# Hybrid encoder trunk: products of constants placed in TensorE's waits, and short column sums spread between long products

## The reference, cut to what matters

```python
kappa = heads(k * k_k)
kh = kappa / jnp.maximum(jnp.sqrt(jnp.sum(kappa * kappa, axis=-1, keepdims=True)), 1e-12)
...
s = (s * w_t[:, :, None, :] - sk[..., None] * (a_t * kh_t)[:, :, None, :]
     + v_t[..., None] * k_t[:, :, None, :])
...
mean = jnp.mean(y, axis=-1, keepdims=True)
var = jnp.mean((y - mean) ** 2, axis=-1, keepdims=True)
y = (y - mean) * lax.rsqrt(var + RW_GN_EPS)
y = y * gn_gain + gn_bias
y = y + jnp.sum(r_h * k_h * r_k, axis=-1, keepdims=True) * v_h
return (y.reshape(bsz, t_len, BRANCH_W) * gate).astype(p.dtype)
```

## Time and profile before

| | |
|---|---|
| median of three runs | 3393.79 us |
| the profiled execution | 3399.08 us |
| its span, first to last instruction | 3397.4 us |
| mean granted clock of TensorE | 0.978 |
| TensorE busy | 3278.0 us (96%) |
| VectorE, ScalarE, GpSimd busy | 1473.5, 1180.7, 1192.4 us |
| DMA | 68 GB/s read from HBM over the span |

### The profile page before, as it was taken

The page is one execution under the profiler, slowest core; times in us unless marked ns, Lnnn a source line. Parts: engine busy times, 40 slices in busy tenths (PEclk is TensorE's granted clock), DMA queues, the critical chain, the costliest instruction groups (busy, mean ns, idle before and its releaser), DMA issues. The chain is left out here.

```text
span 3397.4 us, 72942 instructions
## 1 busy us (share of the span) xinstructions
PE 3278.0 (96%) x29406; PEld 3008.8 (89%) x29406; DVE 1473.5 (43%) x2548; ACT 1180.7 (35%) x2251; POOL 1192.4 (35%) x906
## 2 busy tenths in 40 slices
PE   9999999989899999999999999999898989999997
PEld 8999999977687999999999999999776868888886
DVE  6331155445767334332053312554467673353312
ACT  3222252324554334222242223513245543342222
POOL 4444435200012443444444443351000124545442
PEclk9999999988999999999999999999899999999999
DMA  3333222001121332333233332220021213323332
GB/s 105 90 90 90 82 71 64 6 18 50 41 55 33 89 93 73 90 90 92 74 88 92 90 89 83 66 59 4 18 54 40 58 29 99 87 82 95 93 95 70
DMA packets 464405, 236.48 MB, mean 70 GB/s; under 512 B 20862, under 2 KB 462476, under 8 KB 464156
## 3 DMA queue, kind: packets, MB, share of 16 engines
q1 hardware_dynamic: 464156, 232.92, 24.5%
HBM read 230.50 MB, written 2.10 MB: 68 GB/s over the span
## 5 line engine op out<-in xcount | busy, mean ns | idle before, releaser
L579 POOL TENSOR_TENSOR W_low<-W,W_high 128x512 fp32r<-128x512 f32 (+1 forms) x544 | 723.9, 1332 | 858.6 <-ACT W_high L659 857.9
L155 PE MATMUL PS<-u_high,W_high 128*128 128x264 f32 (+1 forms) x2832 | 864.4, 305 | 5.1 <-ACT vg L2180 1.9
L156 PE MATMUL PS<-u_low,W_high 128*128 128x264 f32 (+1 forms) x2832 | 857.8, 303 | 0.0
L157 PE MATMUL PS<-u_high,W_low 128*128 128x264 f32 (+1 forms) x2832 | 857.6, 303 | 0.0
L659 ACT ACTIVATE W_high<-W 128x512 fp32r<-128x512 f32 (+1 forms) x544 | 336.5, 620 | 984.7 <-PE PS L157 936.0
L155 PEld LDWEIGHTS PS<-u_high,W_high 128*128 128x128 f32 x2832 | 533.1, 188 | 32.4 <-issue 6.3
L156 PEld LDWEIGHTS PS<-u_low,W_high 128*128 128x128 f32 x2832 | 533.6, 188 | 21.6
L157 PEld LDWEIGHTS PS<-u_high,W_low 128*128 128x128 f32 x2832 | 531.6, 188 | 21.7
L155 PE MATMUL PS<-u_high,dW_high 128*128 128x264 f32 (+1 forms) x1344 | 407.2, 303 | 9.0 <-POOL dW_low L1752 4.6
L157 PE MATMUL PS<-u_high,dW_low 128*128 128x264 f32 (+1 forms) x1344 | 385.5, 287 | 0.0
L156 PE MATMUL PS<-u_low,dW_high 128*128 128x264 f32 (+1 forms) x1344 | 385.2, 287 | 0.0
(11 more groups left out here) (399 smaller groups left out, 5359.6 us busy)
## 6 DMA issues: line engine op xcount, KB each, us to landing
W<-in_ffn_w_in SPq DMA_DIRECT2D x352, 256.0 KB, 2.9
dW<-in_w_in SPq DMA_DIRECT2D x172, 256.0 KB, 2.9
W<-in_ffn_w_out SPq DMA_DIRECT2D x160, 256.0 KB, 2.8
W<-in_w_in SPq DMA_DIRECT2D x80, 256.0 KB, 3.0
W<-in_w_branch SPq DMA_DIRECT2D x48, 256.0 KB, 2.9
W<-in_w_out SPq DMA_DIRECT2D x32, 256.0 KB, 2.8
W<-in_ffn_w_out SPq DMA_DIRECT2D x32, 128.0 KB, 2.2
xt<-in_x SPq DMA_DIRECT2D x4, 512.0 KB, 4.8
```

The lines of the kernel that those rows point to most:

```text
L155: nc.tensor.matmul(dst, wh, xh, start=first, stop=False)
L156: nc.tensor.matmul(dst, wh, xl, start=False, stop=False)
L157: return nc.tensor.matmul(dst, wl, xh, start=False, stop=final)
L579: g.tensor_tensor(WL[:, r, 0:nk], W[:, r, 0:nk], WH[:, r, 0:nk].bitcast(F32), ALU.subtract).then_inc(S("split"), 1)
```

## The change

`token_sums` can issue one feature tile at a time, and RWKV's projections put two blocks of the input projection behind each of the first three tiles of sums; 14 blocks follow instead of 20. In the recurrence a new helper `occupy(bank, count)` issues products ones x ones of 128 columns into an unused part of a bank: two, three and three in the step of the last chunk, twice three in the last step, and four behind the loop. RWKV's output has the squares two by two around the first bonus sum, and four products ones x ones ahead of the wait for the root. The FFN that ends layer 0 gets five of them as well.

```diff
--- before.py
+++ after.py
@@ -174,9 +174,9 @@
                     sp.sem_clear(range(numbers[0], numbers[-1] + 1))
             named.clear()
 
-        def token_sums(src, weights, nw):
-
-            for m in range(4):
+        def token_sums(src, weights, nw, tiles=range(4)):
+
+            for m in tiles:
                 for j, (t0, n) in enumerate(ST_):
                     c = 4 * nw * j + nw * m
                     last = nc.tensor.matmul(PS[0:n, 0, c:c + nw], src(m)[:, t0:t0 + n], weights, start=True, stop=True)
@@ -647,7 +647,10 @@
                             pe.wait_ge(S("out_put"), KD - 3)
                             nextp.turn(pe, PS[:, 0])
                         early_sums(pe)
-                        if not nextp:
+                        if nextp:
+                            for _ in range(5):
+                                nc.tensor.matmul(PS[:, 1, 0:P], ones[:], ones[:], start=True, stop=True)
+                        else:
                             lead.occupy(pe, 5)
 
                     @block.scalar
@@ -1194,8 +1197,12 @@
                     dense.blocks(pe, 4)
                     pe.wait_ge(S("kappa_squares"), 1)
                     pe.wait_ge(S("sigmoid"), 8)
-                    token_sums(lambda m: s4[:, m], per_parity, 2).then_inc(S("kappa_sums"), 1)
-                    dense.blocks(pe, 20)
+                    for m in range(4):
+                        last = token_sums(lambda m: s4[:, m], per_parity, 2, (m,))
+                        if m < 3:
+                            dense.blocks(pe, 2)
+                    last.then_inc(S("kappa_sums"), 1)
+                    dense.blocks(pe, 14)
                     for m in range(4):
                         spread_out(m)
                         dense.blocks(pe, 8)
@@ -1522,6 +1529,12 @@
                                 last = product(zps[:, m], carry[:, m, 1], carry[:, m, 0], CH, CH)
                         last.then_inc(S("carry2_made"), 1)
 
+                    def occupy(bank, count):
+
+                        for _ in range(count):
+                            nc.tensor.matmul(PS[:, bank, 384:512], ones[:], ones[:], start=True, stop=True,
+                                             skip_group_check=True)
+
                     for g in range(NG + 1):
                         p, makes, steps = g - 1, g < NG, g > 0
                         whole, was_whole = makes and LEN[g] == CH, steps and LEN[p] == CH
@@ -1533,12 +1546,18 @@
                             read(p)
                         if makes:
                             reach_grams(g)
+                        if g == NG:
+                            occupy(0, 3)
                         if steps:
                             first_solution(p)
+                        if g == NG:
+                            occupy(0, 3)
                         if makes:
                             squares(g)
                         if was_whole:
                             second_solution(p)
+                        if g == NG - 1:
+                            occupy(7, 2)
                         if makes:
                             fourths(g)
                         if was_whole:
@@ -1548,8 +1567,12 @@
                             eighths(g)
                         if steps and makes:
                             new_state(p)
+                        if g == NG - 1:
+                            occupy(3, 3)
                         if makes:
                             inverses(g)
+                        if g == NG - 1:
+                            occupy(3, 3)
                         if steps:
                             if not was_whole:
                                 pe.wait_ge(S("x0"), g)
@@ -1561,6 +1584,7 @@
                         if whole:
                             carries(g, 1)
                             double_carries(g)
+                    occupy(0, 4)
             clear()
             rec.close()
             with nc.Block() as block:
@@ -1665,10 +1689,14 @@
 
                     for m in range(4):
                         sums(y[:, m], half_ones[:], m, "sum_y")
-                    for m in range(4):
-                        squares(m)
+                    squares(0)
+                    squares(1)
                     bonus(0)
+                    squares(2)
+                    squares(3)
                     bonus(1)
+                    for _ in range(4):
+                        nc.tensor.matmul(PS[:, 6, 0:P], ones[:], ones[:], start=True, stop=True, skip_group_check=True)
                     pe.wait_ge(S("var_rsqrt"), 1)
                     spread_out(0)
                     pe.wait_ge(S("bonus_out"), 1)
```

## The result

The kernel after takes 3400.3 us (median of 20 runs), the kernel before 3391.4 us in 20 runs of its own. One run of each took far longer (5125.57 and 4341.32 us) and stays out of the ratio; the others lie between 3393.2 and 3406.0, and between 3388.1 and 3399.6. The ratio is 1.0022 with a 95% interval of 1.0016 to 1.0028: slower by 7.5 us (5.4 to 9.5). The forecast was 3382, and its range ended at 3395.

What follows compares the result with a forecast made beforehand. TensorE, busy 96% of the span, was taken to bound the kernel, with its clock at half in places. Terms -4.8 - 0.5 + 2.2 + 0.4 - 3.6 + 1.2 - 6.4 - 0.4 = -11.9 us off the 3393.79 median gave 3382, range 3371 to 3395.

Steps and rivals of the forecast that it cites:

- Kappa: RWKV's projections: sums spread among input-projection blocks keep the clock full, -4.8 us for both layers, bounds 0 and -4.8.
- Stage change: Layer 0 to layer 1: five constants add about 0.9 us, full clock gains 1.5; net -0.5 us.
- Constants inside the recurrence: Last chunk: eight products, gross 1.7 us per layer, partly absorbed by starved issue; +2.2 us for both layers.
- Constants in the last step: Recurrence's last step: twice three products hidden in waits for ScalarE's copy but for 0.1 each; +0.4 us for both layers.
- Outputs of the last step: Recurrence's end: 48 records run at full instead of half clock, 1.8 us gained per layer; -3.6 us for both.
- closing constants: Four products behind the recurrence's loop take 0.86 us, the following gap shrinks; +1.2 us for both layers.
- Sums of y: RWKV's output: sixteen records take 3.5 us at full clock instead of 6.67; -6.4 us for both layers.
- Squares and bonus: RWKV's output: reordered squares and constants before the root gain little, as the clock may fall; -0.4 us for both layers.
- rival (c): Only kappa and stage change hold; at the recurrence's end constants delay the clock's fall: +4.2 us, 3398, chance 0.20.
- Rival (b): RWKV's output: the squares hold the clock as well, another 2.45 us gained per layer; 3377, chance 0.20.
- (d): Everywhere edited: light work between does not matter for the clock, constants bring no return; +10.4 us, 3404, chance 0.07.
- (e): Gains come but about 5 us are lost to longer half-clock stretches at the next phase's start or later; 3387, chance 0.08.

Runs made afterwards that it cites:

- the tail constants: Kernel before plus only twice three products of constants in the recurrence's last step and four behind its loop: ratio 1.0005, 3394.25 us.
- the tail held: Kernel before plus spread kappa sums, stage-change constants, last-step and closing constants, and two more between the halves of the last outputs: 1.0004, 3390.54 us.
- the output's constants: Kernel before plus only four products of constants ahead of the wait for the root in RWKV's output: ratio 1.0009, 3396.83 us.
- the pair: Kernel before plus spread kappa sums and the five stage-change constants, nothing at the recurrence's end or in RWKV's output: 0.9995, 3388.66 us.
- parted squares: Kernel before plus seven products of constants behind each of the first three groups of squares in RWKV's output: single run, 3401.8 us.

## Why the prediction was wrong

Fourteen profiles, each with two layers, let every term be read many times over. The table gives the mean of each piece, without and with its edit, and the difference for both layers (for the stage change, once), beside the forecast. In brackets the number of cases; a kernel with only a part of a piece's edit, or with another one there, is left out of its row. The pieces: kappa from its first sum to its first spreading product; stage change from the first transpose to the first long product; last chunk from its first square to the last step's read of the state, last step from there to the first output; outputs to the first sum of y, the closing constants included; y sums to the first squares; from there to the next phase's first product.

| piece | without, us | with, us | measured | forecast |
|---|---|---|---|---|
| kappa | 21.67 (20) | 19.00 (8) | -5.3 | -4.8 |
| stage change | 10.78 (10) | 10.39 (4) | -0.4 | -0.5 |
| last chunk | 9.22 (22) | 10.82 (6) | +3.2 | +2.2 |
| last step | 2.25 (20) | 2.84 (6) | +1.2 | +0.4 |
| last outputs, closing constants | 3.91 (20) | 4.21 (6) | +0.6 | -3.6 + 1.2 = -2.4 |
| sums of y | 6.09 (20) | 5.75 (6) | -0.7 | -6.4 |
| squares to next phase | 22.70 (18) | 25.73 (4) | +6.1 | -0.4 |
| sum | | | +4.7 | -11.9 |

The sum is below the timed 7.5 (5.4 to 9.5). The missing 2.8 us lie in no piece that I can name; the part of the recurrence ahead of the last chunk varies between 113.5 and 116.7 us in all profiles, edited or not, which is enough to hide them. Nor is the sum exact: the six cases behind the sums of y alone spread from 3.6 to 6.7 us, and by the spread of the cases I estimate some 2.5 us either way for the whole sum.

The forecast missed the sum of the pieces by 16.6 us. Two steps failed. One is the assumption that the constants at the recurrence's end keep the clock up through the last outputs and the sums of y: -2.4 and -6.4 forecast, +0.6 and -0.7 measured, 8.7 us. The other is the term for squares and bonus, -0.4 forecast and +6.1 measured, 6.5 us and the largest miss of one piece.

**Kappa** was right in mechanism, place and size. The eight cases with spread sums are within 0.02 us of 19.00. The twenty without are 20.5 (3.4 us at half) or 21.9 to 22.0 (6.8 us), with 16 of the longer kind.

**Stage change** was right in size, less so in its reasons. Seven of ten executions without the constants have only 3.4 us at half there, and take the same 10.3 to 10.4 us as those with them. Only where 6.8 us are at half (11.84) do the constants return anything. The profile of before was of this rarer kind, so the mean agrees with the forecast by luck. Profile against profile, after against before, the change is 11.84 to 10.35 us, -1.5: up to the next stage's first product it is 1.3 us longer (forecast 0.9), from there to the first long product 2.8 shorter (9.31 to 6.52, forecast 1.5).

**Constants inside the recurrence** were undersized. The forecast let idle "issue" time absorb a third of 1.7 us per layer. Measured is 1.6 on the mean, the gross price. The single cases vary by as much (8.0 to 10.8 us without, 10.4 to 11.7 with), so that nothing is absorbed is likely, not shown.

**Constants in the last step** too: 0.1 was forecast for each group of three, 0.3 measured (2.25 to 2.84 us for both). Timeline of after, last step, layer 0:

```profile
720.27 0.94 PE L1535 MATMUL PS<-ones 128*128 128x128 f32 x6
721.14 0.62 PE L1365 MATMUL PS<-xr,inv 16*16 16x64 f32 x16
721.69 0.94 PE L1535 MATMUL PS<-ones 128*128 128x128 f32 x6
722.56 0.29 PE L1365 MATMUL PS<-reach,tk 16*64 16x16 f32 x4
...
724.79 1.56 PE L1535 MATMUL PS<-ones 128*128 128x128 f32 x8
```

Three constants take 0.87 us from their first record to the next work's (720.27 to 721.14), not the 0.64 of six records at 0.107, and the pause they stand in was 0.6.

**Outputs of the last step**: a gain of 1.8 us per layer was read off one profile. In 8 of the 20 cases without the constants these outputs are at full clock anyway (3.27 to 3.39 us to the first y sum, mostly 4.0 to 4.5 otherwise). And the full-clock price was taken from 64-row outputs, 1.54 us; the 16-row ones take 2.23 (722.56 to 724.79, above). So some 1.1 us was to be had, in 12 of 20 cases, and the closing constants cost 0.8 in every case: at full clock throughout, the piece takes 4.09 us with them and 3.28 without.

**Sums of y** came to -0.7 against -6.4. The forecast took it that the clock stays up, hence 3.5 us. In one of six cases it did (3.64 us); the other five have 6.17 on the mean, no gain at all. In those five the fall only came later: among the closing constants or in the pause behind them, 2.8 to 3.5 us behind the first output, instead of in the outputs, and the sums of y then ran at half. What made the one case different no run shows. This is the forecast's rival (c), "delay the fall but don't prevent it", and it had a chance of 0.20.

**Squares and bonus** had the wrong sign. The text itself said that here the short sums outweigh the long products more than two to one, and then took -0.2. The new order makes the second stretch 10.24 us in all six cases that have it (before, 3.4 or 6.8): +2.1 us per layer on the mean. The four constants add 0.93 like for like (21.80 to 22.74, 23.25 to 24.18, 24.80 to 25.73), because the bonus sums last until the root is there at either level, so that nothing is left to cover. That is close to 8 records at full clock, 0.86, though they take 1.9 at half: the stretch's length does not grow with them, so I take it that other work moves out of it. (The forecast's terms for this piece at full clock also add up to 7.1, not 6.9.)

The sum of rival (c) was +4.2, near the +4.7 of the pieces, with its own terms off both ways: it had the closing constants and sums of y at +3.5 (measured -0.1), and the output's constants at +3.4 where order and constants together make +6.1. Rival (b) is refuted by the squares, (d) by kappa. Of (e) the profile of after shows nothing: the next phase's start is at half for 17.06 us in both layers, as before. But four of the other 26 cases have 20.5 us there (the tail constants and the tail held in layer 0, the output's constants and the pair in layer 1). Window of the pair, layer 1, columns as in the earlier trace rows:

```profile
2438.40:2458.80 20.40, 16.36 (x55) 11.83 (x56) 7.65 (x12) 6.79 (x13) 0.00 (x0) 0.50 0.40 104
```

The two profiles with it in layer 0 take 945.0 and 945.1 us from that phase's first product to the stage change, the kernel before 942.6 and 942.7 in its two executions. So some 2.4 us of a gain can be lost there; whether an edit brings it about or chance does, no run here tells.

The Trainium skill's rule on idle gaps, weighed in the prediction (page "TensorE: Matmul & The Clock Gate", section "Why this matters for your kernels"), comes out better in its consequence than in its cause. Constants were indeed nearly all cost at the recurrence's end. But idle gaps alone do not explain it: the kernel with parted squares kept the clock through a stretch in which TensorE was busy without a pause, and the one with only a new order was at half for 10.24 us where others have 3.4 or 6.8, equally busy. The kind of work matters.

**Best version.** Kappa alone, 0.9988 (0.9978 to 0.9999), is the only kernel that measured faster than the kernel before clear of noise, and that barely; with the stage change it is 0.9995 (0.9985 to 1.0005), and the two intervals overlap. I would keep kappa and leave the rest out.

## What to carry to other kernels

Before you price a half-clock stretch, profile the same program two or three times, and give each stretch the mean of what it takes: here kappa, the stage change, the last outputs, the sums of y and the squares each varied by 1.1 us or more between executions that had no edit there, and the profile at hand happened to be an unfavourable one. Spreading light work among heavy work that exists anyway added no instruction, and at the kappa sums it held the clock in eight of eight cases. Buying heavy work (products of constants) showed a clear gain nowhere: where TensorE had no wait it cost its full time, three products of 0.64 us in a wait of 0.5 cost 0.3, and even where it held the clock it cost more than it gave. A reordering has a price too, though it adds nothing: the new order of the squares cost 4.4 us. When a forecast's own text says which side a case is nearer to, let the number follow it.

## What the runs showed that I had not expected

The half-clock stretches come in few lengths: 3.4, 6.8, 10.2, 13.7, 17.1 and, in four profiles, 20.5 us are all that I measured here. This makes stage times jump by steps (kappa 19.0, 20.5, 22.0; the output 21.8, 23.3) rather than scatter, and a span carries the sum of many such draws (18 stretches in the profile of after, ahead of the last product): 19 of the 20 runs of the kernel before spread over 3388 to 3400 us. The recurrence's 3 us of variation at full clock come on top.

Forty loads of 128 columns with products of 2 columns take 4.43 us at full clock; twenty take 2.20 at full and 3.79 at half in the rows of after above. So here the work made of loads slows by 1.72, not by 2.
